# Second layer's mixer of a two-block transformer kernel: turns placed between projections, one gain folded into another, a fused bias-add and maximum, and another order inside the attention steps

## Chip, cores and metric

The kernel runs on one core of a Trainium2 chip. The metric is the device time of one execution in microseconds; the time before is 2416.76 us, the median of three runs (2415.67 to 2419.11 us).

## The reference, cut to what matters

The reference computes two transformer blocks one after the other, each of two layers, over 256 tokens of width 1024, all in fp32. The change touches one place: the mixer of layer 1 of the first block (`odd_mixer`).

```
def odd_project(h, w_in, q_g, k_g):         # for the tokens x and for the context
    q, k, v = split(h @ w_in)               # 16 heads of 64
    return rms_norm(q, q_g), rms_norm(k, k_g), v

# na_latent: for each head and each query
#   near = q . k(x) / 8 + bias(relative position)   256 keys
#   far  = q . k(context) / 8                       256 keys
#   p    = softmax([near, far])
#   y    = p[near] @ v(x) + p[far] @ v(context)
x = x + g_a * (y @ w_out[1])
```

`odd_project` is written out here from what the kernel computes: three projections of the normed input, an RMS norm by head of q and of k, each with a gain of 64 values. What follows (the feed-forward part of layer 1 and the second block) is long and untouched.

## The kernel before, in words

Nearly all time goes to matrix products in fp32 precision, made of three reduced-precision passes: each operand is split into a high part and a low remainder, and `product` (lines 507 to 509) issues high by high, high by low and low by high. The weights come in a fixed order as chunks of 1 MB through a ring of four slots. SyncE issues each chunk's DMA when the chunk four places before is used up; ScalarE makes the high part (line 1190, a ring of three), VectorE the low part (line 1639). In ScalarE's and VectorE's programs the places of these splits are written out by hand (`split_for`, `lo_for`, `lo_to`): a chunk is split when the engine comes to that line, not when the data is there.

The stages around the change, in the order of TensorE's program:

- `project_tok("od_q", ...)`: the query, 2 column blocks of 512, 4 chunks, 24 matmuls a chunk. VectorE copies each block from PSUM to `nq` (`store`, line 1935).
- `project_tok("od_kv", ...)`: key and value for x and context, 4 blocks (two of key into `nk_`, two of value into `nv`), 8 chunks of 48 matmuls, each block in two groups with one pair of PSUM banks each (banks 0 to 3, reused from block to block: a block's first group waits until VectorE has stored the same pair of the block before).
- Between these stores VectorE norms `nq` and then `nk_` (`group_rms`; `rms_sums` at lines 1742 and 1743, `rms_scale` at 1751 to 1756): squares, sums by head, reciprocal of the root from ScalarE (line 1279), product with it, product with the gain.
- `pre_turn "na"` (line 2098) is sent when all this is done. Then TensorE turns (transposes) `nq` in 8 blocks of 2 tiles and `nk_` in 8 blocks of 4 tiles through banks 4 to 7 (line 654); ScalarE copies the high part out (line 1211), VectorE the low part (line 1660). The turned key's high part lands in `x_hi`, which the projections read until their last matmul.
- The bias by relative position comes in two DMA groups of four (2 MB each, `rel_in`), issued by SyncE (line 1145) in front of the third chunk of `w_out`: group 0 (heads 0 to 7) goes into `free_b`, the place of `x_lo`, and so waits for the last projection; group 1 goes into the place of `nk_` and waits for its last turn.
- `attend_pairs`: 16 units (8 pairs of heads, 2 query tiles). TensorE: `scores(u)` (line 745, 6 matmuls, two banks), `turn_probs(u, i)` (line 755, 4 transposes each), `values(u)` (line 765, 16 matmuls). VectorE: `maxes(u)` (for each head the bias is added in PSUM over 256 keys, line 1836, then the maximum over 512, line 1838), `norms(u)` (reciprocal of the sum, line 1845, and scaling of the probabilities, line 1847), `outs(u)` (split of the result into high and low, lines 1664 and 1665). ScalarE: `exps(u)` (line 1323, with the sum as accumulator output) and `copy_probs(u)` (line 1331). Step u of the loop holds turn 0 of u, scores of u+2, turn 1 of u and values of u-1 on TensorE.
- `w_out` follows at once on the last values.

## Time and profile before

| what | value |
|---|---|
| median of three runs | 2416.76 us |
| profiled execution, its own time | 2416.47 us |
| its span in the profile | 2414.7 us |
| TensorE matmul busy | 2304.4 us, 95% |
| weight load (beside the matmuls) | 1985.0 us, 82% |
| VectorE busy | 1503.6 us, 62% |
| ScalarE busy | 1013.3 us, 42% |
| mean granted TensorE clock | 0.982 |
| chain that ended last | TensorE 84%, VectorE 8%, ScalarE 4%, DMA 2%, issue 2% |

TensorE is busy nearly everywhere, so time can only be won where it waits, or where other work stands on the chain in its place. The profile's own numbers are microseconds from the start of the span; 1.77 us of the profiled execution lie outside the span.

### The profile page before, as it was taken

The page shows a single profiled execution, that of the slowest core. Times are in us where ns is not written, and L with a number is a line of the kernel's source. Part 1 is how long each engine was busy: PE and PEld are TensorE (multiplying, and loading weights), DVE is VectorE, ACT ScalarE, POOL GpSimd, SP SyncE. Part 2 cuts the span into 40 slices and gives each one's busy share as a digit, 9 for nine tenths or more (in the row PEclk, how much of TensorE's full clock was granted, in tenths as well). Part 3 has the DMA queues.
Part 4 walks back from the last instruction along what each step waited for, and adds up shares of the span by engine and source line. Part 5 has one row for each costly group of instructions (what it writes and reads, how often), then busy time and mean ns, then how long its engine had stood idle before and what let it go on. Part 6 is the DMA issues. An engine that isn't in the chain of part 4 may idle for free.

```text
span 2414.7 us, 33051 instructions
## 1 busy us (share of the span) xinstructions
PE 2304.4 (95%) x14198; PEld 1985.0 (82%) x14198; DVE 1503.6 (62%) x1866; ACT 1013.3 (42%) x1226; POOL 0.2 (0%) x4
## 2 busy tenths in 40 slices
PE   6988989999998887999999999999999999999997
PEld 3765767777876756999999877999989988789997
DVE  3777443333356577555678767675668767767475
ACT  4255441111224155434664345443456534444343
POOL 0000000000000000000000000000000000000000
PEclk9999999999998999999999999999999999999999
DMA  8530134444332241455555453555545445445552
GB/s 324 206 143 1 54 137 176 177 172 181 133 117 93 87 105 71 158 184 192 216 191 187 174 193 143 179 188 176 189 177 205 179 174 197 148 175 177 190 176 104
DMA packets 61401, 389.19 MB, mean 161 GB/s; under 512 B 6600, under 2 KB 11080, under 8 KB 16072
## 3 DMA queue, kind: packets, MB, share of 16 engines
q1 hardware_dynamic: 61256, 387.08, 44.0%
q8 instruction: 112, 1.84, 0.3%
q14 instruction: 33, 0.27, 0.0%
HBM read 386.01 MB, written 1.05 MB: 160 GB/s over the span
## 4 chain that ended last, share of the span: by engine, by line
PE 84%; DVE 8%; ACT 4%; DMA 2%; issue 2%; SPq 0%; DVEq 0%; ACTq 0%
PE PS L507 26%; PE PS L508 25%; PE PS L509 25%; DMA raw<-chunks_in 2%; PE PS L815 1%; PE PS L984 1%; DVE w_lo L1639 1%; ACT w_hi L1190 1%; DVE stat L1838 1%; PE PS L694 1%; PE PS L966 1%; ACT xn L1268 1%; PE PS L654 1%; PE PS L719 1%; DVE BIG L1847 1%
## 5 line engine op out<-in xcount | busy, mean ns | idle before, releaser
L1639 DVE TENSOR_TENSOR w_lo<-raw,w_hi 128x2048 fp32r<-128x2048 f32 x300 | 683.5, 2290 | 514.4 <-ACT w_hi L1190 512.5
L1190 ACT ACTIVATE w_hi<-raw 128x2048 fp32r<-128x2048 f32 x300 | 571.7, 1912 | 755.7 <-PE PS L509 453.3
L507 PE MATMUL PS<-x_hi,w_hi 128*128 128x256 f32 (+1 forms) x2048 | 629.0, 307 | 12.2 <-DVE x_lo L1704 7.8
L509 PE MATMUL PS<-x_hi,w_lo 128*128 128x256 f32 (+1 forms) x2048 | 626.1, 306 | 0.0
L508 PE MATMUL PS<-x_lo,w_hi 128*128 128x256 f32 (+1 forms) x1984 | 601.5, 303 | 0.0
L507 PEld LDWEIGHTS PS<-x_hi,w_hi 128*128 128x128 f32 x2048 | 393.6, 192 | 38.5 <-issue 21.8
L509 PEld LDWEIGHTS PS<-x_hi,w_lo 128*128 128x128 f32 x2048 | 393.6, 192 | 16.7
L508 PEld LDWEIGHTS PS<-x_lo,w_hi 128*128 128x128 f32 x1984 | 381.7, 192 | 14.1
L507 PE MATMUL PS<-w_hi,x_hi 128*128 128x512 f32 (+1 forms) x800 | 318.5, 398 | 23.2 <-DVE x_lo L1704 12.0
L508 PE MATMUL PS<-w_lo,x_hi 128*128 128x512 f32 (+1 forms) x800 | 314.5, 393 | 0.0
L509 PE MATMUL PS<-w_hi,x_lo 128*128 128x512 f32 (+1 forms) x800 | 313.9, 392 | 0.0
L507 PE MATMUL PS<-BIGR,w_hi 128*128 128x256 f32 (+1 forms) x896 | 272.8, 304 | 0.0
L508 PE MATMUL PS<-BIGR,w_hi 128*128 128x256 f32 (+1 forms) x896 | 272.3, 304 | 0.0
L509 PE MATMUL PS<-BIGR,w_lo 128*128 128x256 f32 (+1 forms) x896 | 272.3, 304 | 0.0
L507 PEld LDWEIGHTS PS<-w_hi,x_hi 128*128 128x128 f32 x800 | 152.6, 191 | 63.2 <-issue 18.8
L507 PEld LDWEIGHTS PS<-BIGR,w_hi 128*128 128x128 f32 x896 | 171.3, 191 | 10.4 <-issue 3.6
L509 PEld LDWEIGHTS PS<-w_hi,x_lo 128*128 128x128 f32 x800 | 152.5, 191 | 31.8
L508 PEld LDWEIGHTS PS<-w_lo,x_hi 128*128 128x128 f32 x800 | 152.6, 191 | 29.7
L509 PEld LDWEIGHTS PS<-BIGR,w_lo 128*128 128x128 f32 x896 | 171.3, 191 | 6.9
L508 PEld LDWEIGHTS PS<-BIGR,w_hi 128*128 128x128 f32 x896 | 171.3, 191 | 6.7
L507 PE MATMUL PS<-w_hi,BIGR 128*128 128x512 f32 x192 | 75.7, 394 | 0.0
L509 PE MATMUL PS<-w_hi,BIGR 128*128 128x512 f32 x192 | 74.8, 390 | 0.0
(298 smaller groups left out, 2281.2 us busy)
## 6 DMA issues: line engine op xcount, KB each, us to landing
raw<-chunks_in SPq DMA_DIRECT2D x348, 1024.0 KB, 4.8
bias_ring<-brows_in SPq DMA_DIRECT2D x32, 256.0 KB, 5.1
G<-nrows_in SPq DMA_DIRECT2D x2, 1536.0 KB, 6.6
free_b<-rel_in SPq DMA_DIRECT2D x4, 512.0 KB, 7.8
BIG<-rel_in SPq DMA_DIRECT2D x4, 512.0 KB, 8.7
tabt<-tabs_in SPq DMA_DIRECT2D x1, 1536.0 KB, 12.6
X<-x_in SPq DMA_DIRECT2D x1, 1024.0 KB, 8.7
X<-ctx_in SPq DMA_DIRECT2D x1, 1024.0 KB, 10.7
```

What stands on the lines that cost most here:

```text
L507: pe.matmul(o, lhs[0], rhs[0], start=start, stop=False, **more)
L508: pe.matmul(o, lhs[0], rhs[1], start=False, stop=False, **more)
L509: return pe.matmul(o, lhs[1], rhs[0], start=False, stop=stop, **more)
L654: mm = pe.transpose(PS[:, bank, t * P:(t + 1) * P], src(b, t), ident)
L694: mm = pe.matmul(PS[:, s + i, 0:d["nk"]], a, b, start=m == 0, stop=m == len(mats) - 1)
L719: mm = pe.matmul(PS[:, b, 0:P], pT_, val, start=j == 0, stop=j == n - 1)
L815: mm = pe.matmul(PS[32 * kt:32 * kt + 32, b, :], cond[:, 4 * kg + kt, at:at + 32], w[:, kt, :], start=first, stop=i == last and kg == 1, s ...
L966: mm = pe.matmul(PS[:, b, cols], qkT[:, 8 + 2 * h + j, s * P:(s + 1) * P], qkT[:, 2 * h + j, s * P:256], start=j == 0, stop=j == 1)
L984: mm = pe.matmul(PS[:, 6 + t, 0:dv], lhs, val[:, s, h * dv:(h + 1) * dv], start=s == 0, stop=s == len(blocks) - 1)
L1190: act.activation(w_hi[:, i % HI_RING, :], ring[:, n % RING, :], ACT.Copy).then_inc(*hi_ready.now(n))
L1268: ins = act.activation(o, o, ACT.Identity, bias=modc[l][:, kind * 8 + k, w:w + 1], scale=modc[l][:, kind * 8 + 8 + k, w:w + 1])
L1639: dve.tensor_tensor(w_lo[:, c % RING, :], ring[:, c % RING, :], w_hi[:, i % HI_RING, :].bitcast(F32), ALU.subtract).then_inc(*lo_ready.now(c))
```

## The change

TensorE turns the query right after key block 1, and the key after value block 0 (`od_kv` block 2), so that both turns stand between projections; the last projection comes after them. For this the turned key's high part goes to the `xn` region and the attention's output to the `x_hi` region; bias group 0 takes the place of `nk_` (waits for the last key turn) and group 1 that of `free_b` (waits for the last projection). Their DMAs stand in front of the second and of the third `w_out` chunk. The squares of `nq` and `nk_` move from VectorE to ScalarE. The key's gain is multiplied into the query's once, in the small gain table, and the product of `nk_` with its gain goes away. In the attention, a unit's maximum is made of one reduction over both heads' 256 far keys and two `tensor_tensor_reduce` (bias add with running maximum, each with an accumulator output), and one tiny negation; the two reciprocals become one; the high copy of the output moves to ScalarE. TensorE issues scores of u+2 ahead of both turns of u, and VectorE's order is maxes(u+2), norms(u+1), outs(u-2).

```
-        v["nkT"] = pair_of((xhi_, G_r), 512, 8)
-        v["rel"] = [free_b[:, :]..., big(2048, 4096)...]
+        v["nkT"] = pair_of((xnr_, G_r), 512, 8)
+        v["rel"] = [a.rearrange(...) for a in (big(2048, 4096), free_b[:, :])]
-        yT_na = pair_of((xnr_[:, 0:2048], xnr_[:, 2048:4096]), 256, 8)
+        yT_na = pair_of((xhi_[:, 0:2048], xhi_[:, 2048:4096]), 256, 8)
...  TensorE, attend_pairs
                 for u in range(len(us)):
-                    turn_probs(u, 0)
                     if u + 2 < len(us):
                         scores(u + 2)
+                    turn_probs(u, 0)
                     turn_probs(u, 1)
...  TensorE
-            project_tok("od_kv", 1, 4, KD, tokens(hT[4]), 2)
-            pe.wait_ge(*pre_turn.after("na"))
+            project_tok("od_kv", 1, 2, KD, tokens(hT[4]), 2)
+            pe.wait_ge(*pre_turn.after("naq"))
             turn("naq", 8, 2, ...)
+            project_tok("od_kv", 1, 1, KD, tokens(hT[4]), 2, n0=2)
+            pe.wait_ge(*pre_turn.after("nak"))
             turn("nak", 8, 4, ...)
+            project_tok("od_kv", 1, 1, KD, tokens(hT[4]), 2, n0=3)
...  SyncE
-                if c == first("w_out", 1) + AHEAD:
-                    for part in range(2):
-                        if part == 0:
-                            sp.wait_ge(*projected.after("od_kv", 1, 3, 1))
-                        else:
-                            sp.wait_ge(*turned.after("nak", 7))
+                for part in range(2):
+                    if c == first("w_out", 1) + 1 + part:
+                        sp.wait_ge(*(projected.after("od_kv", 1, 3, 1) if part else turned.after("nak", 7)))
...  ScalarE, attend_pairs
+                def copy_out(u):
+                    pair, q = us[u]["out"]
+                    act.wait_ge(*attended.after("na", u))
+                    act.activation(yT_na[0][:, pair, q], PS[:, pair_banks(u)[2], 0:P], ACT.Copy).then_inc(*copied_s.now("na", u))
                 for u in range(len(us)):
                     copy_probs(u)
                     if u + 2 < len(us):
                         exps(u + 2)
+                    if u >= 1:
+                        copy_out(u - 1)
+                copy_out(len(us) - 1)
...  ScalarE
             split_for("od_q", 1, 1)
+            act.wait_ge(*stored.after("od_q", 1, 1, 0))
+            act.activation(xn_[:, 0:2048], nq..., ACT.Square).then_inc(*squared.now("naq"))
             root("naq", 32, 64)
             split_for("od_kv", 1, 1)
+            copy_turned("naq")
+            act.wait_ge(*stored.after("od_kv", 1, 1, 1))
+            act.activation(xn_[:, :], nk_..., ACT.Square).then_inc(*squared.now("nak"))
             root("nak", 64, 64)
+            split_for("od_kv", 1, 2)
+            copy_turned("nak")
             split_for("od_kv", 1, 3)
-            copy_turned("naq")
-            copy_turned("nak")
...  VectorE, attend_pairs
+                    k = 192 + 2 * (u % 4)
+                    link(dve.tensor_reduce(stat[:, k:k + 2], PS[:, s:s + 2, 256:512], AX_X, ALU.max))
                     for i in range(2):
                         near = PS[:, s + i, 0:256]
-                        link(dve.tensor_tensor(near, near, us[u]["bias"][:, i, :], ALU.add))
-                        dve.tensor_reduce(stat[:, k:k + 1], PS[:, s + i, :], AX_X, ALU.max, negate=True)...
+                        ins = dve.tensor_tensor_reduce(near, near, us[u]["bias"][:, i, :], 1.0, stat[:, k + i:k + i + 1], ALU.add, ALU.max,
+                                                       stat[:, k + i:k + i + 1])
+                    link(ins)
+                    dve.tensor_scalar(stat[:, k:k + 2], stat[:, k:k + 2], -1.0, None, ALU.mult).then_inc(...)
                 def norms(u):
+                    dve.wait_ge(*exp_ready.after("na", u, 1))
+                    link(dve.reciprocal(stat[:, r:r + 2], stat[:, o:o + 2]))
                 def outs(u):
-                    split([a[:, pair, q] for a in yT_na], PS[:, pair_banks(u)[2], 0:P])...
+                    dve.wait_ge(*copied_s.after("na", u))
+                    dve.tensor_tensor(lo, PS[:, pair_banks(u)[2], 0:P], hi.bitcast(F32), ALU.subtract)...
                 maxes(0)
-                norms(0)
                 maxes(1)
-                norms(1)
+                norms(0)
                 for u in range(len(us)):
                     if u + 2 < len(us):
                         maxes(u + 2)
-                    if u >= 1:
-                        outs(u - 1)
-                    if u + 2 < len(us):
-                        norms(u + 2)
+                    if u + 1 < len(us):
+                        norms(u + 1)
+                    if u >= 2:
+                        outs(u - 2)
+                outs(len(us) - 2)
                 outs(len(us) - 1)
...  VectorE, early
+            link(dve.tensor_tensor(row("na_q_g"), row("na_q_g"), row("na_k_g"), ALU.mult))
...  VectorE
-            group_rms("naq", nq..., xn_, [(0, 16, row("na_q_g"))])
+            group_rms("naq", nq..., xn_, [(0, 16, row("na_q_g"))], by_act=True)
+            link(dve.memset(small[:, 16:17], 0.0), pre_turn, "naq")
-            store("od_kv", 1, 2, 2, kv_view)
-            dve.wait_ge(stored.sem, stored.count)
+            store("od_kv", 1, 1, 2, kv_view)
+            store("od_kv", 1, 1, 2, kv_view, 1)
+            copy_turned("naq")
-            rms_sums("nak", nak, xn_)
-            lo_to(place_of[plan["last chunk", "od_kv", 1, 1]] + AHEAD + 1)
-            rms_scale("nak", nak, [(0, 16, row("na_k_g"))])
-            store("od_kv", 1, 2, 2, kv_view, 2)
-            link(dve.memset(small[:, 16:17], 0.0), pre_turn, "na")
-            copy_turned("naq")
+            rms_sums("nak", nak, xn_, by_act=True)
+            rms_scale("nak", nak, [])
+            link(dve.memset(small[:, 16:17], 0.0), pre_turn, "nak")
+            store("od_kv", 1, 1, 2, kv_view, 2)
             copy_turned("nak")
+            store("od_kv", 1, 1, 2, kv_view, 3)
```

## Rows read from the trace of the kernel before

**Rows 1.** Stretches: length; busy (count) of PE, PEld, DVE, ACT, POOL; clock; DMA.
```profile
806.65:828.20 21.55, 21.55 (x96) 17.64 (x94) 18.98 (x7) 4.07 (x3) 0.00 (x0) 1.00 0.28 98
...
858.00:868.50 10.50, 6.98 (x49) 5.07 (x48) 8.89 (x18) 8.11 (x17) 0.00 (x0) 1.00 0.91 183
...
870.60:934.30 63.70, 50.27 (x473) 35.09 (x471) 58.61 (x158) 41.80 (x97) 0.00 (x0) 0.96 0.24 63
```

**Rows 2.** The chain that ended last, 806 to 873: start, length, what.
```profile
833.22 1.15 DVE BIG L1935
...
835.27 0.43 PE PS L508
...
860.31 10.27 DMA free_b<-rel_in
```

**Rows 3.** VectorE's instructions in order of time, before the attention.
```profile
807.91 4.42 DVE L1742 TENSOR_TENSOR xn<-BIG 128x4096 f32<-128x4096 f32 x1
...
863.58 4.87 DVE L1660 TENSOR_TENSOR G_r<-PS,x_hi 128x512 fp32r<-128x512 f32 x8 [0.39 <-ACT x_hi L1211]
```

**Rows 4.** TensorE in order of time: last projection's start, the turns, the first scores.
```profile
834.50 0.77 PE L507 MATMUL PS<-w_hi,x_hi 128*128 128x512 f32 x1 [6.13 <-DVE BIG L1935]
...
859.44 1.09 PE L654 MATMUL PS<-tabt,BIG 128*128 128x128 f32 x8 [1.34 <-DVE small L2098]
860.89 5.89 PE L654 MATMUL PS<-tabt,BIG 128*128 128x128 f32 x40 [0.35 <-DVE SCR_r L1660]
868.56 0.76 PE L745 MATMUL PS<-x_hi,BIGR 64*128 64x512 f32 x2 [1.78 <-DVE G_r L1660]
```

**Rows 5.** SyncE's DMA issues in order of time.
```profile
858.20 2.75 SPq L1145 DMA_DIRECT2D free_b<-rel_in  x4
```

**Rows 6.** The page's costliest groups: ScalarE's split of a weight chunk.
```profile
L1190 ACT ACTIVATE w_hi<-raw 128x2048 fp32r<-128x2048 f32 x300 | 571.7, 1912 | 755.7 <-PE PS L509 453.3
```

**Rows 7.** One step of the attention on VectorE, in order of time.
```profile
885.44 0.43 DVE L1836 TENSOR_TENSOR PS<-PS,free_b 128x256 f32<-128x256 f32 x1
885.90 0.69 DVE L1838 TENSOR_REDUCE stat<-PS 128x1 f32<-128x512 f32 x1
...
887.89 0.29 DVE L1665 TENSOR_TENSOR xn_r<-PS,xn_r 128x128 fp32r<-128x128 f32 x1
888.10 0.15 DVE L1845 RECIPROCAL stat<-stat 128x1 f32<-128x1 f32 x1
888.29 0.49 DVE L1847 TENSOR_SCALAR BIG<-BIG,stat 128x512 f32<-128x512 f32 x1
888.69 0.16 DVE L1845 RECIPROCAL stat<-stat 128x1 f32<-128x1 f32 x1
...
889.28 0.42 DVE L1836 TENSOR_TENSOR PS<-PS,free_b 128x256 f32<-128x256 f32 x1
```

**Rows 8.** TensorE through two attention steps, in order of time.
```profile
882.54 0.66 PE L755 MATMUL PS<-tabt,BIG 128*128 128x128 f32 x4
883.13 0.50 PE L745 MATMUL PS<-x_hi,BIGR 64*128 64x512 f32 x2
...
884.61 1.09 PE L765 MATMUL PS<-X,BIG 128*64 128x128 f32 x16
885.63 0.66 PE L755 MATMUL PS<-tabt,BIG 128*128 128x128 f32 x4
```

**Rows 9.** Groups of ScalarE's instructions, shapes apart, 866 to 935.
```profile
L1323 ACT ACTIVATE BIG<-PS,stat 128x512 f32<-128x512 f32 x32 | 22.0, 687 | 23.5 <-DVE stat L1838 23.5
L1331 ACT ACTIVATE X<-PS 128x512 f32<-128x512 f32 x32 | 17.2, 592 | 0.3 <-PE PS L755 0.3
L1323 ACT ACTIVATION_READ_ACCUMULATOR BIG<-PS,stat 128x1 f32 x32 | 6.2, 193 | 0.0
```

**Rows 10.** Groups of VectorE's instructions, shapes apart, whole span.
```profile
L1725 DVE SCALAR_TENSOR_TENSOR x_lo<-X,colt,x_hi 128x256 fp32r<-128x256 f32 x48 | 22.7, 480 | 3.8 <-ACT x_hi L1225 3.8
```

**Rows 11.** VectorE's first instruction behind the small gain products, in order of time.
```profile
59.82 2.29 DVE L1639 TENSOR_TENSOR w_lo<-raw,w_hi 128x2048 fp32r<-128x2048 f32 x1 [5.27 <-ACT w_hi L1190]
```

More of the change, by code:

```diff
@@ L1474, in _ @@
             split_for("od_q", 1, 1)
+            act.wait_ge(*stored.after("od_q", 1, 1, 0))
+            act.activation(xn_[:, 0:2048], nq.rearrange("p t c -> p (t c)"), ACT.Square).then_inc(*squared.now("naq"))
             root("naq", 32, 64)
             split_for("od_kv", 1, 1)
+            copy_turned("naq")
+            act.wait_ge(*stored.after("od_kv", 1, 1, 1))
+            act.activation(xn_[:, :], nk_.rearrange("p t c -> p (t c)"), ACT.Square).then_inc(*squared.now("nak"))
             root("nak", 64, 64)
+            split_for("od_kv", 1, 2)
+            copy_turned("nak")
             split_for("od_kv", 1, 3)
-            copy_turned("naq")
-            copy_turned("nak")
             attend_pairs()
@@ L1841, in norms @@
+                    link(ins)
+                    dve.tensor_scalar(stat[:, k:k + 2], stat[:, k:k + 2], -1.0, None, ALU.mult).then_inc(*max_ready.now("na", u, 0))
+                    max_ready.alias("na", u, 1)
                 def norms(u):
+                    o, r = 200 + 2 * (u % 4), 208 + 2 * (u % 4)
+                    dve.wait_ge(*exp_ready.after("na", u, 1))
+                    link(dve.reciprocal(stat[:, r:r + 2], stat[:, o:o + 2]))
                     for i in range(2):
-                        o, r = 200 + 2 * (u % 4) + i, 208 + 2 * (u % 4) + i
@@ L1844, in norms @@
-                        dve.wait_ge(*exp_ready.after("na", u, i))
-                        link(dve.reciprocal(stat[:, r:r + 1], stat[:, o:o + 1]))
                         p = probs["na"][:, u % 2, i, :]
-                        dve.tensor_scalar(p, p, stat[:, r:r + 1], None, ALU.mult).then_inc(*probs_ready.now("na", u, i))
+                        dve.tensor_scalar(p, p, stat[:, r + i:r + i + 1], None, ALU.mult).then_inc(*probs_ready.now("na", u, i))
                 def outs(u):
                     pair, q = us[u]["out"]
-                    dve.wait_ge(*attended.after("na", u))
@@ L1852, in outs @@
-                    split([a[:, pair, q] for a in yT_na], PS[:, pair_banks(u)[2], 0:P]).then_inc(*y_out.now("na", u))
+                    dve.wait_ge(*copied_s.after("na", u))
+                    hi, lo = (a[:, pair, q] for a in yT_na)
+                    dve.tensor_tensor(lo, PS[:, pair_banks(u)[2], 0:P], hi.bitcast(F32), ALU.subtract).then_inc(*y_out.now("na", u))
                 maxes(0)
+                maxes(1)
                 norms(0)
-                maxes(1)
-                norms(1)
```

8 lines of the change are left out of this document (2 added, 6 removed).

## The prediction

> **What bounds the kernel now.** I read the page first: TensorE is 95% busy, so I looked for the places where it is not, and where the chain that ended last leaves it. Then the busy time by stretch, the chain from 806 to 873 us, and the engines' instructions in order of time. Three things stand on the path around this mixer.
>
> First, the last projection of key and value starts late. Block 2 ends at 828.3 by its pace (96 matmuls in 21.55 us [rows 1]), but block 3 starts only at 834.50, after 6.13 us of waiting for VectorE's store [rows 4], which ends at 834.37 by the chain [rows 2]: VectorE was still in the norm of the key, whose passes over 4096 columns take 4.42 us each [rows 3]. Behind the wait the clock is at its lower level (1.2 of 2.4 GHz): the first matmul takes 0.77 us [rows 4], and about eight follow each other at 0.43 us [rows 2] where 21.55/96 gives 0.22, 1.7 us more. Block 3 therefore ends at 858.1 (834.5 + 21.6 + 1.7 = 857.8, and the chain's next link starts right behind).
>
> Second, from there to the first scores at 868.56 TensorE does only the 48 turns, 1.34 us late, and waits 1.78 us for the last low copy [rows 4]; then the first bias add waits for the bias, whose DMA is issued at 858.20 [rows 5] and lands at 870.58 [rows 2].
>
> Third, from 870.6 to 934.3 VectorE is busy 58.6 of 63.7 us, TensorE 50.3 [rows 1]. One VectorE step runs from 885.44 to 889.28 without a gap: 3.84 us [rows 7]. TensorE with nothing to wait for does its step in 885.63 - 882.54 = 3.09 us [rows 8]. So VectorE is the bound of this loop, by 0.75 us a step.
>
> **The sum is made against the profiled execution**, 2416.47 us (span 2414.7), 0.29 us under the median of the runs. About 0.2% (4.8 us) is what a measurement can tell from no change.
>
> **1. Turns between the projections.** The query's turn comes at 806.6, when block 1 ends (one block before 828.2 [rows 1]). Is its data ready? The query's norm is over by some 775 (its store is long done, and it is three passes of half 4.42, one of them now ScalarE's): 30 us of cover. Its cost on TensorE: all 48 turns took 7.3 us (859.44 to 860.89 + 5.89 [rows 4]), and the key's part is bounded by VectorE's eight low copies, 4.87 us [rows 3]; so the query's is about 2.6 us. Now VectorE is also storing block 1's second group for 1.2 us (a store is 1.15 [rows 2]) when the turns begin, so I take 3.0. Block 2 then runs 809.6 to 831.2. The key's turn: ScalarE squares `nk_` after the query's copies, about 810.3, in twice 1.91 us [rows 6]; reduce 4.42, root and reciprocal about 1 us, one product 4.42 [rows 3], so `pre_turn` comes at about 824, against 831.2: 7 us of cover. Had the squares and the gain stayed on VectorE (4.42 each, 0.6 of the first won by ScalarE's pace), it would be 829, and then the cover is nearly gone. Turning it costs TensorE 4.5 us (the four last blocks wait for VectorE's copies at 0.61 each, behind a store of 1.2 us). Block 3 runs 835.7 to 857.3, at full clock, with no stall: the store of block 2's first group is at 829.9, behind two low splits of 2.3 us that start at 824. The scores start at 857.4 instead of 868.56. In sum: the stall and its slow clock go (-7.8), the turns move in front of block 3 (+7.5), the 10.5 us behind it go [rows 1], together with 0.3 of rounding: **-11.1 us**.
>
> **2. The bias.** Group 0 waits for the last key turn, 835.7, is issued by 838.5 (2.75 us for four [rows 5]) and lands 10 to 11 us later, at 849; wanted at 858.5. So the first VectorE instruction comes one scores phase (1.0 us) behind 857.4, not 2.05: **-1.0 us**. What is queued behind this wait on SyncE is the second `w_out` chunk, which came some 5 us earlier: it lands near 850, its high split 1.9 [rows 6] and low split 2.3 us end at 854.3, in front of the store of block 3's first group (done at 852), and the second store is at 857.3 anyway. Nothing is late, with 3 us to spare. Group 1 is issued at 857.4 to 860.2, lands at 870 and is wanted in unit 8, past 881. The third `w_out` chunk behind it lands before 875 and is wanted after 920.
>
> **3. The loop.** TensorE's work in a step is the same: 0.59 + 0.89 + 0.59 + 1.09, 3.1 us [rows 8]. VectorE's new step, by starts in rows 7 (an instruction that is waited for costs its length and 0.04, one that isn't about 0.08 less than its length): one reduction over 512 elements, waited for, 0.73; two fused adds with maximum; a tiny negation, 0.10; one reciprocal 0.19; two scalings 0.81 (twice 888.69 - 888.29); one subtraction 0.21. Without the fused ones: 2.04.
>
> The fused operation is in no row. From below: an add of 256 is 0.42 long, about 0.36 start to start by that rule of starts. With a pointer operand the same size takes 0.480 [rows 10], 0.40 start to start. An accumulator output is a read behind the main instruction on ScalarE, 0.193 us [rows 9], of which about 0.10 is not overlapped. I take 0.40 + 0.10 = 0.50 (the nearest rows), 0.04 more for the second, which is waited for: the step is 2.04 + 1.04 = **3.08 us**, just under TensorE's 3.1. From above: twice the streaming time of 0.27 added, 0.77 each, 3.6 us a step. Below 0.36 it can't win anything, for TensorE is then the bound.
>
> That an operation with an accumulator output is two instructions, the main one and a read, is also what the Trainium skill states for VectorE ("VectorE: DVE Perf Modes", Two Vector instructions with no wait between them); the trace shows it for ScalarE alone.
>
> ScalarE: two exponentials 0.68 each, two copies 1.07 together (lengths in [rows 9], the next starting about 0.1 before the end), one 128x128 copy, at most 0.3: 2.7 us, under the bound. The loops through all engines (probabilities scaled, turned, copied, next exponentials, scaled) add to about 3.9 us over two steps, so none binds; putting the scores ahead of both turns gives VectorE its input 0.6 us earlier.
>
> Start and end: maxes of 0 and 1 take 2 x 1.87 from 858.5, then reciprocal and one scaling 0.6: first turn at 862.8. From there TensorE has 13 scores (0.89), 32 turns (0.59) and 16 values (1.09): 47.9 us. I add 0.9 for waits while the pipe fills and empties, and 1.0 for the clock: TensorE idles 2 to 3 us before the first turn, as it did in front of 868.56, where the first scores took 0.76 instead of 0.50 [rows 4, 8]. Last values end at 912.6; before, `w_out` starts at 934.3. That is 54.1 us from the first VectorE instruction, against 63.7: **-9.6 us**.
>
> **4. Edits at nothing.** The gain product in the small table (about 0.2 us) stands early, and VectorE idles 5.27 us right behind it [rows 11]. Squares on ScalarE fall into its idle time (755.7 us in front of its splits alone [rows 6]). If the split of key chunk 6 came later than 827, block 3 would wait; it is at 821. The third chunk's split behind the last output copy on ScalarE has 11 us until TensorE wants it.
>
> **Sum:** 11.1 + 1.0 + 9.6 = 21.7 us; 2416.47 - 21.7 = **2394.8 us**. Everything behind is a dense chain of TensorE and shifts as a whole.
>
> **Rivals.**
>
> (a) *VectorE stays the bound*, because the fused operation takes 0.65 to 0.8 us. Each 0.1 us more on it is 0.2 us in each of some 15 steps, 3.1 us. At 0.77 the step is 3.6, the loop 7.5 us longer: 2402.5. For it: no row has the operation, and VectorE's step is within 0.02 us of TensorE's. Against: a two-input operation with a pointer is not slowed, 0.480 for 256 elements [rows 10].
>
> The Trainium skill has a rule that speaks for (a): by "Vector Engine (DVE) Microarchitecture Reference", Points that are easy to get wrong, the scalar-tensor-tensor shape with two non-bf16 SBUF sources has half the throughput, since no port is left for the accumulator. Here one source is PSUM; if it held all the same, the sum would be that of (a), 2402.5; rows 10, two SBUF sources in fp32 without accumulator output, do not show it.
>
> (b) *The front is late*: chunk and bias DMAs queue on each other, or the key's norm misses 831, and scores start 2 to 5 us later: 2397 to 2400. For it: SyncE is in order and group 0's wait now stands before a chunk. Against: 3 and 7 us of cover.
>
> (c) *Slower or no change*: one mechanism, the fused operation is far dearer than any built-in one, for instance through a fixed cost at each call. The place is VectorE's step. The gain of 21.7 is gone when VectorE's step reaches 3.1 + 21.7/15.5 = 4.5 us, so when the fused operation takes (4.5 - 2.04)/2 = 1.2 us; at 1.4 us it is 6 us slower than before, 2423. The longest VectorE instruction of comparable size is 0.69 for 512 elements, so this is unlikely.
>
> (d) *The turns cost more than they hide*: if each of the two turns brought the lower clock as the wait before block 3 did, 1.7 us each: 2398.2. Waits there are around 1 us, and the 1.34 us wait at 859.44 left the clock at 1.00 [rows 1].
>
> **Chances.** Forecast, TensorE bounds the loop, 2391.5 to 2398: 0.68. (a) 0.17, (b) and (d) 0.09, no change 0.03, slower 0.03. Range: down to 2391.5 (no fill waits, no slow clock, 1 us less in the turns), up to 2403.5, which takes in (a), (b) and (d). Faster 0.94, same 0.03, slower 0.03.
>
> **What would show it.** TensorE's idle in front of block 3 gone, its first matmul at 0.39; two groups of turns near 807 and 831, about 3.0 and 4.5 us; first scores near 857; no wait on the bias; fused operation near 0.48 long with a short read behind it; step 3.1 to 3.2 us; `w_out` from about 913. A step above 3.3 with VectorE without gaps means (a); a wait of TensorE on `pre_turn` or a weight split between 806 and 860 means (b). The prediction is wrong if the fused operation has another length than 0.35 to 0.55, or if TensorE waits in steady steps though no engine is full.

## The result, and the profile after

The changed kernel takes 2389.93 us (median, 2388.90 to 2391.97 us) beside 2416.23 us for the kernel before on the same chip: ratio 0.989, 95% interval 0.9878 to 0.9902, 26.3 us less. The forecast was 2394.8 us in a range from 2391.5 us: the sign is right, the gain is larger than forecast and the median lies 1.6 us under the range. The profiled execution took 2391.97 us (span 2390.2), 24.5 us less than that of before, and this is what the sum stands against.

The page of the changed kernel, busy time of each engine and the chain by engine:

```profile
PE 2298.6 (96%) x14198; PEld 1981.6 (83%) x14198; DVE 1479.4 (62%) x1865; ACT 1020.5 (43%) x1244; POOL 0.2 (0%) x4
...
PE 86%; DVE 7%; ACT 4%; issue 2%; DMA 2%; SPq 0%; DVEq 0%; ACTq 0%
```

VectorE lost 24 us of work, ScalarE gained 7, and TensorE's share of the chain rose by two points. TensorE in order of time from the end of key block 1 to `w_out` (start, length, instruction, the wait before it in brackets):

```profile
807.25 1.03 PE L653 MATMUL PS<-tabt,BIG 128*128 128x128 f32 x8
809.06 1.43 PE L653 MATMUL PS<-tabt,BIG 128*128 128x128 f32 x8 [0.78 <-DVE SCR_r L1672]
810.25 0.48 PE L506 MATMUL PS<-w_hi,x_hi 128*128 128x512 f32 x1
...
832.15 1.91 PE L653 MATMUL PS<-tabt,BIG 128*128 128x128 f32 x16
834.22 2.45 PE L653 MATMUL PS<-tabt,BIG 128*128 128x128 f32 x16 [0.17 <-DVE G_r L1672]
836.43 0.48 PE L506 MATMUL PS<-w_hi,x_hi 128*128 128x512 f32 x1
...
858.41 0.50 PE L744 MATMUL PS<-xn_r,BIGR 64*128 64x512 f32 x2
...
863.17 0.80 PE L744 MATMUL PS<-xn_r,BIGR 64*128 64x512 f32 x2 [3.09 <-ACT BIG L1322]
...
864.75 1.97 PE L754 MATMUL PS<-tabt,BIG 128*128 128x128 f32 x8
866.64 0.51 PE L744 MATMUL PS<-xn_r,BIGR 64*128 64x512 f32 x2
...
876.38 1.09 PE L754 MATMUL PS<-tabt,BIG 128*128 128x128 f32 x8
877.40 1.09 PE L764 MATMUL PS<-X,BIG 128*64 128x128 f32 x16
878.42 0.50 PE L744 MATMUL PS<-xn_r,BIGR 64*128 64x512 f32 x2
...
905.84 1.09 PE L754 MATMUL PS<-tabt,BIG 128*128 128x128 f32 x8 [0.85 <-DVE BIG L1862]
...
910.84 0.39 PE L506 MATMUL PS<-x_hi,w_hi 128*128 128x256 f32 x1
```

The stall of 6.13 us in front of block 3 [rows 4] is gone. The query's turns take 810.25 - 807.25 = 3.0 us, the key's 836.43 - 832.15 = 4.3, and both projections behind them start at once. Scores start at 858.41, before at 868.56 [rows 4]. The only long idle time left is 3.09 us in front of the third scores, behind which the first scores matmuls take 0.80 us where they take 0.50 before and after: the lower clock again, granted at 0.50 of full speed to about 866.6.

Busy time by stretch, columns as in rows 1 (the attention, its steady part, block 3):

```profile
859.70:910.80 51.10, 47.16 (x472) 35.34 (x468) 46.23 (x160) 41.91 (x111) 0.00 (x0) 0.97 0.32 84
880.00:904.00 24.00, 24.00 (x246) 17.84 (x246) 23.16 (x81) 20.95 (x58) 0.00 (x0) 1.00 0.01 2
836.40:858.40 22.00, 22.00 (x99) 17.94 (x97) 7.67 (x7) 5.91 (x5) 0.00 (x0) 1.00 0.62 144
```

In the steady part TensorE is busy all the time, VectorE nearly, ScalarE 87%: two engines are full and the third is near it. One VectorE step (CUSTOM_DVE_ANT_0 is the fused add with maximum, followed by the read of its accumulator):

```profile
897.38 0.68 DVE L1847 TENSOR_REDUCE stat<-PS 128x2 f32<-128x512 f32 x1
898.10 0.49 DVE L1850 CUSTOM_DVE_ANT_0 PS<-PS,free_b,stat 128x256 f32<-128x256 f32 x1
898.50 0.14 DVE L1850 DVE_READ_ACCUMULATOR2_ANT stat<- 128x1 f32 x1
898.50 0.49 DVE L1850 CUSTOM_DVE_ANT_0 PS<-PS,free_b,stat 128x256 f32<-128x256 f32 x1
...
899.09 0.17 DVE L1853 TENSOR_SCALAR stat<-stat 128x2 f32<-128x2 f32 x1
899.16 0.16 DVE L1859 RECIPROCAL stat<-stat 128x2 f32<-128x2 f32 x1
899.35 0.88 DVE L1862 TENSOR_SCALAR BIG<-BIG,stat 128x512 f32<-128x512 f32 x2
900.15 0.28 DVE L1868 TENSOR_TENSOR x_hi<-PS,x_hi 128x128 fp32r<-128x128 f32 x1
900.35 0.68 DVE L1847 TENSOR_REDUCE stat<-PS 128x2 f32<-128x512 f32 x1
```

It takes 900.35 - 897.38 = 2.97 us, before 3.84 [rows 7]. TensorE's own work in a step is 2.94 (0.90 for the scores, 1.02 for eight turns, 1.02 for the values, 876.38 to 878.42 for the last two), so VectorE is the slower by 0.03, and from 870.6 to 905.8 the chain that ended last runs through VectorE. TensorE does not feel it at first: its slow start has put it behind VectorE, and from 869.59 to 901.94 it does eleven steps at its own 2.94 without a wait. What VectorE is slower by shows only at the end, within the 0.85 us in front of unit 14's turns (905.84).

**Where the 24.5 us came from.** VectorE's last store of key block 1 begins at 806.65 before (the start of rows 1) and at 807.45 after. From there to VectorE's first work of the attention (870.6 and 859.66): 63.96 and 52.21 us, **11.8 less**. From there to the first `w_out` matmul (934.3 and 910.84): 63.7 and 51.2, **12.5 less**. Together the stretch shrinks from 127.63 to 103.39 us, 24.2 less, and what is behind it shifts as a whole, within 1.1 us (1480.4 and 1479.4 us to the end of the span). The experiments below are read by this stretch, from their profiles, because it leaves out what the untouched rest of the kernel does from run to run: over the 14 profiles the time outside the stretch goes from 2286.1 to 2291.6 us.

### The profile page after: what moved, and what is told of

Its sections match the earlier page's. It is cut to its first block, busy times and chain, and to the rows that moved or that the text cites. A ratio compares the mean times of both kernels' runs of the same rounds, so it can differ in the third digit from the quotient of the medians.

```text
span 2390.2 us, 33070 instructions
## 1 busy us (share of the span) xinstructions
PE 2298.6 (96%) x14198; PEld 1981.6 (83%) x14198; DVE 1479.4 (62%) x1865; ACT 1020.5 (43%) x1244; POOL 0.2 (0%) x4
## 4 chain that ended last, share of the span: by engine, by line
PE 86%; DVE 7%; ACT 4%; issue 2%; DMA 2%; SPq 0%; DVEq 0%; ACTq 0%
PE PS L506 26%; PE PS L507 26%; PE PS L508 26%; PE PS L986 1%; PE PS L814 1%; DMA raw<-chunks_in 1%; DVE w_lo L1651 1%; PE PS L693 1%; ACT w_hi L1189 1%; PE PS L968 1%; PE PS L653 1%; ACT xn L1267 1%; PE PS L718 1%; DVE PS L1850 0%; DVE G L1686 0%
## 5 line engine op out<-in xcount | busy, mean ns | idle before, releaser
L506 PE MATMUL PS<-x_hi,w_hi 128*128 128x256 f32 (+1 forms) x2112 | 646.6, 306 | 12.2 <-DVE x_lo L1716 7.8
L508 PE MATMUL PS<-x_hi,w_lo 128*128 128x256 f32 (+1 forms) x2112 | 643.4, 305 | 0.0
L506 PEld LDWEIGHTS PS<-x_hi,w_hi 128*128 128x128 f32 x2112 | 405.2, 192 | 39.5 <-issue 22.8
L508 PEld LDWEIGHTS PS<-x_hi,w_lo 128*128 128x128 f32 x2112 | 405.2, 192 | 16.7
```

The costliest lines, as they stand in the source:

```text
L506: pe.matmul(o, lhs[0], rhs[0], start=start, stop=False, **more)
L508: return pe.matmul(o, lhs[1], rhs[0], start=False, stop=stop, **more)
```

## The experiments

**The changed kernel again, on two chips.** No edit.

> The changed kernel once more, without an edit, to see how far its time moves by itself. Theory A (the sum missed by the loop's step alone, 2.97 instead of 3.1 us, and the rest of the miss is scatter between executions): again 2388 to 2392 us, 25 to 27 us under the kernel before, w_out starting 24 us earlier than before or so and the work before and behind the mixer within 1.5 us of before in sum. Theory B (the change also wins something behind or before the mixer that the prediction did not count): the stretch from the first w_out matmul to the end is shorter by 1 us or more in this profile too.

> The changed kernel a third time, beside the further version on one chip. From the two sets so far (26.3 and 23.9 us faster than before): 23 to 27 us faster, the mixer's stretch (end of key block 1 to the first w_out matmul) 103.5 to 104.7 us, and the start of that stretch anywhere in 804 to 808 us, since nothing in front of it was changed.

Measured: 2394.16 us beside 2418.09 (0.990, 0.9887 to 0.9914), stretch 104.38; and 2390.87 beside 2418.59 (0.9892, 0.9876 to 0.9909), stretch 102.61. So the gain is 26.3, 23.9 and 27.7 us in three sets, while the stretch lies within 1.8 us. Both expectations missed: the first median lies above 2392 us, the second gain above 27 us and its stretch under 103.5. Theory B is not borne out: from the first `w_out` matmul to the end of the span it is 1480.1 us in the profile that was to test it, 0.3 less than before (1480.4). The stretch starts at 808.10 and 806.55 here, and between 804.2 and 809.6 over all the profiles, though what stands in front of it is nearly the same in all. TensorE in order of time in the first of the two profiles, the fourth scores (unit 3):

```profile
867.29 0.79 PE L744 MATMUL PS<-xn_r,BIGR 64*128 64x512 f32 x2
```

and in the second profile, the third scores (unit 2):

```profile
862.28 0.49 PE L744 MATMUL PS<-xn_r,BIGR 64*128 64x512 f32 x2 [3.09 <-ACT BIG L1322]
```

In the first the third scores come behind the same 3.09 us and the granted clock is 0.50 to about 869.5; in the second it stays at 1.00. This is all of the 1.8 us: from the third scores to the fifth (unit 4) it is 6.42 us in the first set's profile, 7.41 and 5.62 in these two, and from the fifth scores to `w_out` 41.25, 41.26 and 41.26. A difference of 1 us between two stretches can therefore be the clock at the start alone.

**The two halves alone.** One kernel has the changed front with the old `attend_pairs` on all three engines, the other the old front with the new `attend_pairs`.

```diff
# front only                              # loop only
 front: as changed                        front: as before
-attend_pairs (new, 3 engines)            -attend_pairs (old, 3 engines)
+attend_pairs (old, 3 engines)            +attend_pairs (new, 3 engines)
```

> Only the front of the change: turns between the projections, squares on ScalarE, the key's gain in the query's, the moved places and bias DMAs; the attention loop of the kernel before on all three engines. If the two parts are independent, as the prediction's sum has them: 12.1 us faster than before (11.1 + 1.0), about 2404, first VectorE work of the loop at 859 to 860, loop step 3.84. Rival: the old loop starts no earlier in effect, because VectorE, its bound, gets the last store in front of it: 1.2 us less, 11 us.

> Only the loop of the change on the kernel before; stall before the last projection, turns behind it and the wait for the bias stay. By the prediction 9.6 us faster; by the step read in the changed kernel (2.97) and its shorter start and end 12.5 us, about 2404; step 2.97, TensorE's pure step 2.94. Rival (parts not independent): under 9, or over 15.

Measured: front alone 2403.76 us beside 2418.09 (0.9946, 0.9933 to 0.996), stretch 115.87, 11.8 less than before. Loop alone 2403.10 (0.9942, 0.9929 to 0.9954), stretch 115.39, 12.2 less. The sum, 24.0, is what both give together, 24.2: by the stretch the halves are independent. The medians are too coarse to say so: they give 14.3 and 15.0 us, and 23.9 for both together in the same set; what is over does not lie in the stretch. Within the front, the two parts were not run apart, but the profiles have them: from the start of the stretch to the first scores 61.91 us before and 50.96 after, 10.95 less (forecast 11.1), from there to VectorE's first work 2.05 and 1.25, 0.8 less (forecast 1.0). With the loop alone VectorE's first work still waits for the bias, its DMA being in the old place (VectorE in order of time):

```profile
869.95 0.69 DVE L1843 TENSOR_REDUCE stat<-PS 128x2 f32<-128x512 f32 x1 [2.42 <-DMA free_b<-rel_in]
```

With the front alone that wait is gone, and VectorE goes into the attention from its last store, on which it had waited for TensorE (the same view of that kernel):

```profile
855.94 1.22 DVE L1939 COPY BIG<-PS 128x1024 f32<-128x1024 f32 x1 [0.83 <-PE PS L508]
857.08 0.42 DVE L1840 TENSOR_TENSOR PS<-PS,BIG 128x256 f32<-128x256 f32 x1
```

**The squares and the gain back on VectorE** (key only, both together; the query's squares stay on ScalarE).

```diff
-act.wait_ge(*stored.after("od_kv", 1, 1, 1))
-act.activation(xn_[:, :], nk_..., ACT.Square).then_inc(*squared.now("nak"))
-link(dve.tensor_tensor(row("na_q_g"), row("na_q_g"), row("na_k_g"), ALU.mult))
-rms_sums("nak", nak, xn_, by_act=True)
-rms_scale("nak", nak, [])
+dve.wait_ge(stored.sem, stored.count)
+rms_sums("nak", nak, xn_)
+rms_scale("nak", nak, [(0, 16, row("na_k_g"))])
```

> The changed kernel with the key's squares and its gain product back on VectorE (4.42 us each; ScalarE's squares go). VectorE then has: query copies to 811, squares, reduce, product, gain, so pre_turn of the key at 811.4 + 4 x 4.45 + 1.4 = 830.6, against 832.1 when TensorE wants it: by the prediction's cover no cost there. But two low splits (4.5 us) and the store of block 2's first group stand behind it on VectorE: the splits end at 835.1, the stores at 837.5, the key's low copies at 842.4, so the last projection starts 5 us later than in the changed kernel (836.4): 5 to 7 us slower with the lower clock. Rival: nothing is lost, as a cover of 7 us would say (under 1 us).

Measured: 2398.57 us beside 2418.59 (0.9918, 0.9903 to 0.9932), stretch 108.23, 4.8 and 5.6 us longer than in two profiles of the changed kernel (103.39, and 102.61 on this chip); the median is 7.7 above the changed kernel's on this chip, 2 us of it outside the stretch. VectorE in order of time from the end of the norm:

```profile
832.37 0.06 DVE L2113 MEMSET small<- 128x1 f32 x1
832.47 4.49 DVE L1649 TENSOR_TENSOR w_lo<-raw,w_hi 128x2048 fp32r<-128x2048 f32 x2
836.88 2.35 DVE L1949 COPY BIG<-PS 128x1024 f32<-128x1024 f32 x2
839.14 4.41 DVE L1670 TENSOR_TENSOR G_r<-PS,xn_r 128x512 fp32r<-128x512 f32 x7
```

and TensorE, the second half of the key's turns:

```profile
839.88 3.17 PE L653 MATMUL PS<-tabt,BIG 128*128 128x128 f32 x16 [3.65 <-DVE G_r L1670]
```

The signal for the turn comes at 832.4, just before TensorE wants it (834.3), so the norm itself costs nothing. What comes late is VectorE's work queued behind it: two low splits, two stores, and then the low copies of the turned key, for which TensorE waits 3.65 us in the middle of its turns. The moved squares and gain are worth these 5 us or so.

**The fused operation undone**: the old add, and a maximum over 512 for each head, in the new order.

```diff
-link(dve.tensor_reduce(stat[:, k:k + 2], PS[:, s:s + 2, 256:512], AX_X, ALU.max))
 for i in range(2):
-    ins = dve.tensor_tensor_reduce(near, near, bias, 1.0, ..., ALU.add, ALU.max, ...)
-dve.tensor_scalar(stat[:, k:k + 2], stat[:, k:k + 2], -1.0, None, ALU.mult)
+    link(dve.tensor_tensor(near, near, bias, ALU.add))
+    dve.tensor_reduce(stat[:, k:k + 1], PS[:, s + i, :], AX_X, ALU.max, negate=True)...
```

> The changed kernel with the maximum made as before: for each head a bias add in PSUM (0.46) and a maximum over 512 (0.61). VectorE's step is then 2.97 - 1.79 + 2.14 = 3.32 us and it is the bound: 14 x 0.35 = 4.9 us slower than the changed kernel. Rival: the loop is bound by TensorE and the handovers so that the fused form is worth under 2 us. If the old way of VectorE's first head giving ScalarE its start 0.8 us earlier matters, it is under 4 us.

**The high copy of the output back on VectorE**, with the split as before.

```diff
...  ScalarE: copy_out and its calls go
-act.activation(yT_na[0][:, pair, q], PS[...], ACT.Copy)...
...  VectorE, outs
-dve.tensor_tensor(lo, PS[...], hi.bitcast(F32), ALU.subtract)
+split([a[:, pair, q] for a in yT_na], PS[...])
```

> The changed kernel with the high copy of the attention's output back on VectorE (0.32 us a unit), off ScalarE. VectorE's step 2.97 + 0.32 = 3.29: 14 x 0.32 = 4.5 us slower. Rival: ScalarE, whose step is 2.6 us and which hands on between two TensorE steps, was as near to the bound, and what it wins back makes it under 2.5 us.

Measured, both beside 2417.90 us: unfused 2396.54 (0.9912, 0.9898 to 0.9925), stretch 108.04, 4.65 longer than in the changed kernel; high copy 2397.35 (0.9912, 0.9898 to 0.9925), stretch 107.94, 4.55 longer. The changed kernel was not run in this set; against its other two profiles it is 3.6 to 5.4 us for both. VectorE of the unfused kernel, an add and the same add one step later:

```profile
881.10 0.42 DVE L1848 TENSOR_TENSOR PS<-PS,free_b 128x256 f32<-128x256 f32 x1
...
884.42 0.42 DVE L1848 TENSOR_TENSOR PS<-PS,free_b 128x256 f32<-128x256 f32 x1
```

The step is 3.32 us; with the high copy, from one reduction at 880.42 to the next at 883.72, it is 3.30. The two edits of the change thus take 0.35 and 0.33 us from a VectorE step, and the stretch follows with 13 to 14 steps of each. VectorE bounds the loop with either undone, so each is worth its own cost. A further saving on VectorE was not run. By the trace of the changed kernel it could win, apart from what it takes off the start, at most the 0.85 us for which TensorE waits at the end, since TensorE's own steps are as long as VectorE's but for 0.03. What the other edits in the loop are worth (one reciprocal for two, the reduction over both heads apart from the fused adds) was not run either.

**Orders on TensorE.** First the old place of the scores, between the turns, with VectorE's new order:

```diff
 for u in range(len(us)):
+    turn_probs(u, 0)
     if u + 2 < len(us):
         scores(u + 2)
-    turn_probs(u, 0)
     turn_probs(u, 1)
```

> The changed kernel with TensorE's old order in a step: turn 0, scores of u+2, turn 1, values. Theory A: two turns side by side cost TensorE 1.02 us, and one by one 0.59 each, so the old order's step is 3.09 as in the kernel before, TensorE becomes the bound, and the run is (3.09 - 2.97) x 14 = 1.7 us slower than the changed kernel. Rival: the 3.09 in the kernel before was a wait that the profile does not show, and the step stays at 2.97: same time within 0.5 us. Second rival: VectorE gets its scores 0.6 us later and waits, step above 3.2, 4 us slower.

Measured: 2409.39 us beside 2418.09 (0.9968, 0.9956 to 0.9981), stretch 121.51, 18.1 us longer than in the changed kernel (15.2 by the medians of this set). The second rival had the wait, but 4 us for it; none of the three had a number like that. TensorE in order of time:

```profile
876.57 0.66 PE L754 MATMUL PS<-tabt,BIG 128*128 128x128 f32 x4 [0.96 <-DVE BIG L1862]
877.16 0.50 PE L744 MATMUL PS<-xn_r,BIGR 64*128 64x512 f32 x2
...
880.69 0.66 PE L754 MATMUL PS<-tabt,BIG 128*128 128x128 f32 x4 [0.96 <-DVE BIG L1862]
```

and VectorE of the same kernel:

```profile
876.03 0.88 DVE L1862 TENSOR_SCALAR BIG<-BIG,stat 128x512 f32<-128x512 f32 x2
...
878.16 0.69 DVE L1847 TENSOR_REDUCE stat<-PS 128x2 f32<-128x512 f32 x1 [1.05 <-PE PS L744]
...
879.96 0.16 DVE L1859 RECIPROCAL stat<-stat 128x2 f32<-128x2 f32 x1
```

The step is 880.69 - 876.57 = 4.12 us, and both engines wait in each: a loop through the two. Turn 0 must end before the scores start (0.59), they take 1.00 until VectorE's reduction starts, VectorE needs 1.99 to the start of its scaling (880.15, 0.19 behind the reciprocal), because this stands behind the maxes of the unit just scored, and the next turn 0 waits 0.54 for the first half of it (as from 876.03 to 876.57): 0.59 + 1.00 + 1.99 + 0.54 = 4.12. In the changed kernel the same loop passes over two steps: the values (1.02) and two turns (1.02) stand ahead of the scores, 2.04 + 1.00 + 1.99 + 0.54 = 5.57 us against 5.94, and does not bind.

The next kernel keeps this and also puts VectorE's scaling ahead of the maxes, to break that loop:

```diff
 for u in range(len(us)):
-    if u + 2 < len(us):
-        maxes(u + 2)
     if u + 1 < len(us):
         norms(u + 1)
+    if u + 2 < len(us):
+        maxes(u + 2)
```

> TensorE's old order in a step (turn 0, scores of u+2, turn 1, values), as in the run e3_scores_between, but VectorE does norms(u+1) ahead of maxes(u+2). Theory A, from that run's trace: there a loop through two engines sets the step of 4.12 us (turn 0 of u+1, scores of u+3 behind it, VectorE's maxes of u+3, norms of u+2 behind them, turn 0 of u+2: 0.59 + 0.89 + 1.8 + 0.6 and the handovers). With norms first the loop is open, TensorE's own work with the turns apart is the bound: step 3.09, 1.5 to 2.5 us slower than the changed kernel, some 13 us faster than e3_scores_between. Theory B: the scores' place between the turns costs by itself, whatever VectorE's order: step stays near 4.1.

Measured: 2413.59 us beside 2417.90 (0.998, 0.9971 to 0.9988), stretch 124.83, 3.3 us longer still, and not as either theory had it. VectorE in order of time:

```profile
874.74 0.17 DVE L1859 RECIPROCAL stat<-stat 128x2 f32<-128x2 f32 x1 [1.51 <-ACT BIG L1322]
...
879.14 0.17 DVE L1859 RECIPROCAL stat<-stat 128x2 f32<-128x2 f32 x1 [1.32 <-ACT BIG L1322]
```

and ScalarE, the exponentials between these two:

```profile
877.66 0.69 ACT L1322 ACTIVATE BIG<-PS,stat 128x512 f32<-128x512 f32 x1 [1.81 <-DVE stat L1853]
```

One loop is broken, another is closed, through ScalarE: norms of a unit, maxes of the next (1.00 later), its exponentials (from 877.66), its norms (879.14): 4.40 us a step. VectorE stands still while ScalarE computes what it waits for. In the changed order the maxes of u+2 fill that time. This loop does not pass through TensorE, so it should bind with the scores ahead of both turns too; that kernel was not run.

Last, the turns apart without such a loop: scores first, the values between the turns.

```diff
 turn_probs(u, 0)
-turn_probs(u, 1)
 if u >= 1:
     values(u - 1)
+turn_probs(u, 1)
```

> The changed kernel with the step's order on TensorE: scores of u+2, turn 0, values of u-1, turn 1. The scores stay ahead of both turns, but the turns stand apart. Theory A (what the prediction's 3.09 us was: TensorE's work with the turns apart, each change of kind costing it about 0.07 us): the step is 3.05 to 3.1, bound by TensorE, 14 x 0.1 = 1.5 us slower than the changed kernel. Theory B (the 3.09 held a hidden wait): step 2.97, no difference. Theory C, a loop through the engines again, since the second copy of the probabilities comes 1 us later: step above 3.3, over 4 us slower.

Measured: 2396.57 us beside 2418.59 (0.9911, 0.9896 to 0.9926), stretch 107.52, 4.1 longer (4.9 against the changed kernel's profile of this set, 5.7 by the medians). TensorE has no gap in a steady step, which takes 886.02 - 882.93 = 3.09 us (TensorE in order of time):

```profile
882.93 0.66 PE L754 MATMUL PS<-tabt,BIG 128*128 128x128 f32 x4
883.51 0.50 PE L744 MATMUL PS<-xn_r,BIGR 64*128 64x512 f32 x2
...
886.02 0.66 PE L754 MATMUL PS<-tabt,BIG 128*128 128x128 f32 x4
```

So four turns that stand alone cost TensorE 0.58 to 0.59 us, eight in a row 1.02: the same work is 0.15 us a step dearer when it is apart. That is the 3.09 of rows 8. Theory A had the step; its total, 1.5 us, was too small. The 4.1 us lie in three places: the eleven steps from the fifth scores on, which take 34.0 us for 32.4 (1.7 us); the stretch from the last scores to `w_out`, 10.1 us for 8.9, with two waits of 0.37 and 0.78, the second for the copy of the last unit's second turn (1.2 us); and the start, 1.3 us longer, where the granted clock is 0.50 to about 869 and not to 866.6.

**A version that goes further.** The changed kernel's 3.09 us of idle time and VectorE's slow start can be filled: scores of units 0 and 1 stand between the two chunks of the last projection, their maxes and exponentials ahead of VectorE's and ScalarE's last split of that projection. The second version also puts `norms(1)` there.

```diff
# TensorE
+project_tok("od_kv", 1, 1, KD, tokens(hT[4]), 2, n0=3, between=early)   # early: scores(0), scores(1)
# VectorE
-store("od_kv", 1, 1, 2, kv_view, 3)
-attend_pairs()
+lo_to(place_of[plan["last chunk", "od_kv", 1, 3]] + 1)
+attend_pairs(lambda: store("od_kv", 1, 1, 2, kv_view, 3))   # behind maxes(0), maxes(1), norms(0)
+norms(1)                                                     # second version only, ahead of the stores
# ScalarE
-split_for("od_kv", 1, 3)
-attend_pairs()
+split_to(place_of[plan["last chunk", "od_kv", 1, 3]] + 1)
+attend_pairs(lambda: split_for("od_kv", 1, 3))               # behind exps(0), exps(1)
```

> A further version: the scores of units 0 and 1 are issued between the two chunks of the last projection, so that their maxima, exponentials and the first scaling run beside its second chunk; VectorE stores the last projection behind them. TensorE's 3.1 us of idle in front of the third scores goes, and with it the lower clock behind it (1 to 2 us). Expected: 4 to 5 us faster than the changed kernel, first turn about 3 us behind the last projection instead of 6.3. Rival: VectorE's queue (second low split of w_out, which waits for a chunk until 852, then two stores) holds up maxes of unit 2, and only 1 to 2 us are won. Second rival: the stores of the last projection come late and values of unit 0 wait, no gain.

> The further version v1_early_scores, and the probabilities of unit 1 are scaled ahead of the last projection's stores too. In v1 TensorE still waited 0.89 us for them in front of turn 1 and VectorE then ran without a gap, so 0.9 us off the stretch: 99 us against 103.5 to 104.6 of the changed kernel, 4.5 to 5.5 us faster than it on this chip. Rival: VectorE's wait for ScalarE's exponentials pushes the second low split and the stores back, and the stretch is that of v1, 100 us.

Measured: 2388.44 us beside 2417.90 (0.988, 0.9865 to 0.9895), stretch 99.82; and 2387.73 beside 2418.59 (0.9873, 0.9858 to 0.9888), stretch 98.85. The second is 3.1 us faster than the changed kernel on the same chip (2390.87) by medians and 3.8 by the stretch, under the 4.5 to 5.5 expected: those were reckoned from stretches in which the clock had fallen, and on this chip it had not (102.61). The first has no such pair; its stretch is 3.6 us shorter than that of the first set's profile, expected 4 to 5. In the first, the first unit's turns are followed by a wait for the second's scaling; in the second that is gone. TensorE of the first version:

```profile
862.10 1.09 PE L754 MATMUL PS<-tabt,BIG 128*128 128x128 f32 x8 [0.89 <-DVE BIG L1873]
```

and of the second:

```profile
861.33 0.50 PE L744 MATMUL PS<-xn_r,BIGR 64*128 64x512 f32 x2
...
864.14 1.09 PE L754 MATMUL PS<-tabt,BIG 128*128 128x128 f32 x8
```

With the idle time in front of the third scores gone, these take 0.50 us: no lower clock. What is won, 3.6 and 4.5 us of 103.39, is about the 3.09 us and the clock behind it.

## Why the prediction was right, and where it was wrong

**1, turns between the projections, and 2, the bias: right.** Forecast together 12.1 us, measured 11.8 (both halves together and the front alone). Query turns 3.0 us as forecast, key turns 4.3 for 4.5, scores at 858.41 for 857.4 with a stretch that starts 0.8 later. VectorE of the changed kernel in front of the key's turn:

```profile
814.47 4.42 DVE L1755 TENSOR_REDUCE stat<-xn 128x64 f32<-128x4096 f32 x1 [3.09 <-ACT xn L1488]
...
824.45 0.06 DVE L2115 MEMSET small<- 128x1 f32 x1
```

and ScalarE, the squares ahead of it:

```profile
810.81 3.62 ACT L1488 ACTIVATE xn<-BIG 128x4096 f32<-128x4096 f32 x1
```

ScalarE squares in 3.62 us for the 3.82 taken; the signal comes at 824.45 and TensorE wants it at 832.15, 7.7 us of cover for the 7 forecast. The prediction read that cover as the point of moving the squares and the gain. Its time for the norm with both on VectorE was right: 22.4 us behind the start of the stretch (829), measured 22.7 (832.4 in a profile whose stretch starts 2.2 later), and TensorE wants it 1.9 us after that. What it left out is the work that is queued behind the norm on VectorE: the low copies come late, and that costs the 5 us. The `w_out` chunk behind the bias landed near 852 instead of 850; ScalarE waited 13.0 us for it, and the store behind its splits (856.32) still came before the last one (858.52), so nothing was late (ScalarE's high split):

```profile
852.16 1.92 ACT L1189 ACTIVATE w_hi<-raw 128x2048 fp32r<-128x2048 f32 x1 [13.05 <-DMA raw<-chunks_in]
```

**3, the loop: right in kind, mis-sized.** This is the step that failed: the term "47.9 us" in its sum. From VectorE's first work to `w_out` 54.1 us were forecast and 51.2 measured, so the loop gave 12.5 us and not 9.6. The start was dearer: first turn 5.1 us behind the first work, forecast 4.3. What stood too high is TensorE's work from there. It came from 13 scores at 0.89, 32 turns at 0.59 and 16 values at 1.09. Measured, it is 13 x 0.90 + 16 x 1.02 + 16 x 1.02 = 44.3 us; with 0.85 us of waiting at the end (forecast 0.9) and 0.87 for the clock, in which the first eight turns take 866.64 - 864.75 = 1.89 and not 1.02 (forecast 1.0), that makes the 46.1 us from 864.75 to 910.84. Two terms make up the 3.6 us. The turns: 0.59 was read in rows 8 where each four stand apart, and the change itself puts them side by side, 1.02 for eight; 16 x 0.16 = 2.6 us. The values: 1.09 is their length, while from their start to the next instruction it is 1.02 in the same rows (884.61 to 885.63); 16 x 0.07 = 1.1 us, a slip of reading. Neither of the prediction's own signs of being wrong came up (the fused operation is 0.49 us long, and TensorE waits in no steady step): both looked elsewhere than at this term.

VectorE's step was forecast at 3.08 and is 2.97. The first fused operation gives 898.50 - 898.10 = 0.40 us from start to start, as rows 10 without any read; its accumulator read (0.14 long) starts with the next operation and costs nothing, where 0.10 was taken from ScalarE's reads in rows 9. Only the second one's is waited for. Both cost 0.99 for 1.04, the negation 0.07 for 0.10, and the rest 0.03 less by roundings. Both engines' steps were forecast too long, 3.08 and 3.1 for 2.97 and 2.94, and which of them is the longer came out the other way.

The argument on loops through the engines was true of the order that was built, but it summed one loop alone, 3.9 us over two steps by its figures; the one through the scores and the maxes is 5.57 of 5.94 us, a margin of 0.37. And it said too little: "putting the scores ahead of both turns gives VectorE its input 0.6 us earlier" prices the edit at nothing, while with VectorE's new order it decides between 2.97 and 4.12 us a step, 18 us in all.

**The range.** Of the 4.9 us between forecast and median, 2.5 are the stretch (24.2 for 21.7), 0.3 the rest of the profiled execution's sum, and 2.0 the profiled execution's place over the median of its set. So the mis-sized loop alone does not put the time outside the range: the profiled execution, 2391.97, lies inside, and so does the median of the second set, 2394.16, while that of the third, 2390.87, lies outside. On which side of 2391.5 a set falls is chance; that the forecast was too high is not. The low end left room only for clock, waits and turns (which add to 2.9 us and give 2391.9, not 2391.5), none for the dense step itself, and none for the two to three us either way by which the untouched part moves between profiles. The 2423 us of rival (c) would likewise be 2422 by its own numbers.

**The rivals.** (a), VectorE stays the bound: true in its letter, by 0.03 us a step, at 2.97 and not at 3.6; the fused operation is 0.49 us long, not 0.65 to 0.8. (b), a late front: no wait of TensorE on a signal or a split between 806 and 858. (c), a dear fused operation: no, 0.49 us and not 1.2. (d), lower clock behind the turns: no, block 3's first matmul takes 0.48 us and its stretch has the clock at 1.00; the lower clock comes only behind the 3.09 us of idle time, as forecast for the start.

The rule of the Trainium skill ("Vector Engine (DVE) Microarchitecture Reference", Points that are easy to get wrong) by which the throughput would be halved does not show here, 0.49 us with an accumulator against 0.480 without [rows 10]; but one source is PSUM, and no run has two from SBUF with an accumulator. With what the Trainium skill states of an accumulator output ("VectorE: DVE Perf Modes", Two Vector instructions with no wait between them) this trace agrees, now for VectorE too: two records for each, the main one and a read, 0.49 and 0.14 us long.

## What to carry to other kernels

Before changing the order on one engine, write down for each loop through the engines what stands in front of what on each in-order queue, and add it up per step: TensorE's old order, which cost nothing beside VectorE's old one, made 4.1 us of a step that is 2.97, and the edit on VectorE that was to mend this made 4.4. When work is moved off an engine, look not only at when its result is ready, but at what stands behind it in that engine's queue. Take a dense step's length from starts, not lengths, and from instructions in the order that they will have. Where a pipelined loop must be filled, its first stages can run beneath the work in front of it. And a range should never be narrower than what the untouched part does from run to run.

## What the hardware showed that was not expected

- The read of an accumulator on VectorE (0.14 us) starts together with the next operation, 898.50 for both, so two fused operations follow at 0.40 us; on ScalarE the next operation starts 0.09 us behind the start of the read (862.16 and 862.25).
- Four 128x128 turns between other matmuls cost 0.59 us, eight in a row 1.02: so, as an estimate from these two, a group of turns carries about 0.16 us that does not grow with its number (1.02 - 0.59 is four turns' worth, 0.43). The trace does not show what the engine does in it.
- The same idle time of 3.09 us in front of the third scores was followed by a granted clock of 0.50 to 866.6 in one profile of the changed kernel, to about 869.5 in another, and by none below 1.00 in a third (0.80, 0.80 and 0.49 us for the same two matmuls). With the key's norm on VectorE the wait was 3.10 us and the granted clock was 1.00 to 871.6, more than a microsecond after TensorE had started again (870.21), and 0.50 from 872 on. Over the three profiles of the changed kernel, the way from the third to the fifth scores differs by up to 1.8 us through this alone.
